# Squares of the feed-forward moved to ScalarE, the second layer's decay logits taken ahead of its query tiles, and two operand tiles cast earlier

## The chip, the cores and the metric

The kernel runs on one core of one Trainium2 chip. A core has a matrix engine (TensorE: PE in the profile, with PEld for its weight loads), three engines for elementwise work (VectorE: DVE, ScalarE: ACT, GpSimd: POOL), a queue engine that issues transfers (SyncE: SP), and DMA engines between HBM and the on-chip memories SBUF and PSUM. Each engine works through its own list of instructions in order; semaphores order the engines among each other. The metric is the time of one execution on the device in microseconds (us), lower is better.

## The reference

A sequence of 256 tokens of width 1024 goes through two stacks, in float32. The change is in the first stack alone, which has two layers of this form (the second stack, a Griffin-like and a Mamba-like layer, follows and is not touched):

```
h = layer_norm(ALPHA * h + mixed @ w_out[l], ln1_g[l], ln1_b[l])
ff = jnp.square(jax.nn.relu(h @ w_up[l])) @ w_down[l]
h = layer_norm(ALPHA * h + ff, ln2_g[l], ln2_b[l])
```

`mixed` comes from a mixer over `h @ w_in[l]`: sparse attention, gated linear attention (its decays are a log-sigmoid of small logits that are themselves a product with one tile of `h @ w_in[l]`), and a pooling branch. `w_up` is 1024x4096, `w_down` 4096x1024.

## The kernel before, in words

**Products.** Activations lie transposed, 128 features on the partitions by 256 tokens. Each float32 product is made of three half-precision ones: high weights by high operand, high weights by low operand, low weights by high operand. These are the lines L744, L745 and L746 of `split_matmul`; an output tile of 128 features over 1024 inputs takes 8 x 3 = 24 matmuls. The weights stream from HBM in slots of up to 128x2048 float32. ScalarE writes a slot's high part (`high_part`, L1768), VectorE its low part (`low_part`, L2491), TensorE may then use it (`await_slot`), and SyncE loads the slot four further on (L706). There are four slots in raw form and four in split form, so a high part is made when TensorE has finished the slot four before it. Mostly a slot is a pair of output tiles; in `down1`, whose tiles have 4096 inputs, a pair takes four slots.

**Order of the work.** The order is written out by hand: each engine has its own `first_layer(l)` for the layers l = 0 and 1, and nothing is planned at run time. A layer is the products `in1`, `out1`, `up1`, `down1`, and a layer norm behind `out1` and behind `down1` (numbered m = 0 to 3).

**Raw tiles.** The first four tiles of `up1` and of the second layer's `in1` start before the layer norm's statistics are known: they are computed from the un-normalised sum (`abreast_raw`), whose high part ScalarE makes (`raw_part`, L1808) and whose low part VectorE makes (`raw_low`, L2527). VectorE corrects these tiles in PSUM afterwards (`fix_up`, L2536 to L2548). In `down1`, ScalarE's function `behind(t)` is called after the tile pair of t; its part for t = 6 comes after the high parts of three of the four slots of the last pair. VectorE calls `raw_low` for the tiles 0 to 5 behind its residual addition of tile 5 (L2564), ahead of the low parts of the last pair's last slot and of the first slots of the next product.

**up1.** For each tile ScalarE applies relu from PSUM into `f_relu`, four tiles deep (L2040 for the four raw tiles, L1754 for the others, which wait for `f_ready`, the tile four before). VectorE squares it into the half-precision high part (L2825). GpSimd squares it once more in float32 (L3373), subtracts the high part (L3375), and raises `f_ready`; in between it scales the residual four times (L3350). Behind each pair come a high part on ScalarE and a low part on VectorE.

**Start of the second layer.** TensorE makes the raw tiles, `T_LR` (low rank of the decays, and gates), `T_GK`, `T_GQ + 1` and `T_GQ`, then `T_GV`, the decay logits (`gate_logits`, L1078), `T_GV + 1`, the transposes of the gates (`branch_gates`, L1085, which wait for the evacuation of `T_GQ`), `T_GV + 2`, `T_KC`. VectorE corrects the first two raw tiles, makes the low part of the slot held back, and corrects the other two; then it makes the low part of the slot that holds `T_KC` (`give(0)`) and adds the bias to the logits (L2669). ScalarE evacuates in the same order, makes the high part, and then the log-sigmoid: Abs L1934, Exp L1936, Ln L1939. Its evacuation of `T_GV + 1`, which frees the bank for `T_KC`, comes behind another high part.

## Time and profile before

| what | value |
|---|---|
| median of 3 runs | 1413.29 us (1413.04 to 1414.3) |
| the profiled execution's own time | 1415.02 us |
| its span, first to last instruction | 1413.2 us |
| TensorE busy | 1362.7 us, 96% |
| VectorE busy | 1056.7 us, 75% |
| ScalarE busy | 856.2 us, 61% |
| GpSimd busy | 572.3 us, 40% |
| mean granted TensorE clock | 0.993 of full |

The span is about 1.8 us shorter than the execution's own time. A busy TensorE is not one at its peak: matmuls are pipelined, each is shown with some 0.27 us although the next one starts 0.11 us later, so a stall shows as idle time that is about 0.16 us shorter than the real loss. "PEclk" is the granted clock as a share of 2.4 GHz; 0.50 is the lower of its two levels, 1.2 GHz.

### The profile page before, as it was taken

How to read it: one execution, taken by the hardware profiler on the slowest of the kernel's cores; microseconds unless marked ns; L12 is line 12 of the kernel's file. 1: busy time of each engine (PE TensorE's matmuls, PEld its weight loads, DVE VectorE, ACT ScalarE, POOL GpSimd, SP SyncE). 2: the span in 40 equal slices, each digit the busy share in tenths (PEclk: the TensorE clock that was granted, in tenths of full speed). 3: DMA queues.
4: the chain of work that ended last, by engine and by line, in shares of the span. 5: the costliest groups of instructions: out<-in, count | busy, mean ns of one | idle time of the engine just before them, and what ended most of it. 6: DMA issues, size and time to landing. Idle time of an engine off the chain costs nothing.

```text
span 1413.2 us, 31438 instructions
## 1 busy us (share of the span) xinstructions
PE 1362.7 (96%) x13296; PEld 1162.9 (82%) x13296; DVE 1056.7 (75%) x1465; ACT 856.2 (61%) x1379; POOL 572.3 (40%) x466
## 2 busy tenths in 40 slices
PE   9999999987999999999999999999999999999997
PEld 7778887876778888888777888888887778888887
DVE  6897966547797967558788798865987885898853
ACT  5685444335586544436787566554778888676552
POOL 0154996104144997115220376612222212356620
PEclk9999999999999999999999999999999999999999
DMA  9543556533443456553444265554543333466551
GB/s 360 180 150 121 179 179 226 192 131 105 165 150 121 155 204 209 197 176 106 149 150 170 107 236 196 174 190 150 174 156 124 102 120 122 178 227 217 182 181 31
DMA packets 37020, 234.64 MB, mean 166 GB/s; under 512 B 4752, under 2 KB 7824, under 8 KB 10384
## 3 DMA queue, kind: packets, MB, share of 16 engines
q1 hardware_dynamic: 36880, 232.63, 47.9%
q8 instruction: 105, 1.72, 0.5%
q14 instruction: 35, 0.29, 0.1%
HBM read 231.57 MB, written 1.05 MB: 165 GB/s over the span
## 4 chain that ended last, share of the span: by engine, by line
PE 61%; DVE 16%; POOL 10%; ACT 8%; issue 3%; DMA 1%; ACTq 0%; DVEq 0%; SPq 0%; POOLq 0%
PE psum L744 17%; PE psum L746 17%; PE psum L745 17%; DVE low L2491 5%; POOL arena L3373 4%; POOL arena L3375 4%; ACT high L1768 2%; PE psum L848 1%; PE psum L849 1%; PE psum L850 1%; POOL m L3350 1%; ACT m L2199 1%; PE psum L973 1%; DVE u L2597 1%; DMA raw<-stream 1%
## 5 line engine op out<-in xcount | busy, mean ns | idle before, releaser
L2491 DVE SCALAR_TENSOR_TENSOR low<-raw,high 128x2048 f16<-128x2048 f32 (+5 forms) x247 | 524.5, 2130 | 173.4 <-ACT high L1768 172.8
L744 PE MATMUL psum<-u,high 128*128 128x256 f16 (+2 forms) x1924 | 530.8, 276 | 15.3 <-ACT arena L1754 10.8
L745 PE MATMUL psum<-u,high 128*128 128x256 f16 (+2 forms) x1924 | 530.5, 276 | 0.0
L746 PE MATMUL psum<-u,low 128*128 128x256 f16 (+2 forms) x1924 | 530.4, 276 | 0.0
L1768 ACT ACTIVATE high<-raw 128x2048 f16<-128x2048 f32 (+4 forms) x248 | 418.1, 1690 | 118.4 <-PE psum L746 85.3
L744 PE MATMUL psum<-arena,high 128*128 128x256 f16 (+3 forms) x1208 | 332.8, 276 | 12.4 <-issue 5.3
L745 PE MATMUL psum<-arena,high 128*128 128x256 f16 (+3 forms) x1208 | 332.7, 275 | 0.0
L746 PE MATMUL psum<-arena,low 128*128 128x256 f16 (+3 forms) x1208 | 332.7, 275 | 0.0
L744 PEld LDWEIGHTS psum<-u,high 128*128 128x128 f16 x1924 | 188.4, 98 | 50.9 <-issue 13.7
L745 PEld LDWEIGHTS psum<-u,high 128*128 128x128 f16 x1924 | 188.6, 98 | 28.2 <-issue 0.7
L746 PEld LDWEIGHTS psum<-u,low 128*128 128x128 f16 x1924 | 188.5, 98 | 27.6
L3373 POOL TENSOR_TENSOR arena<-arena 128x256 f32<-128x256 f32 (+1 forms) x108 | 139.8, 1295 | 91.5 <-DVE arena L3002 87.6
L3375 POOL TENSOR_TENSOR arena<-arena 128x256 f16<-128x256 f32 (+1 forms) x108 | 160.6, 1487 | 8.5
L2986 DVE SCALAR_TENSOR_TENSOR arena<-psum,par,arena 128x271 f32<-128x271 f32 (+3 forms) x296 | 143.3, 491 | 22.4 <-ACT arena L2327 9.8
L744 PEld LDWEIGHTS psum<-arena,high 128*128 128x128 f16 (+1 forms) x1208 | 118.9, 98 | 30.7 <-issue 8.6
L745 PEld LDWEIGHTS psum<-arena,high 128*128 128x128 f16 (+1 forms) x1208 | 119.0, 99 | 17.1
L746 PEld LDWEIGHTS psum<-arena,low 128*128 128x128 f16 (+1 forms) x1208 | 119.0, 99 | 16.1
L1754 ACT ACTIVATE arena<-psum 128x256 f32<-128x256 f32 (+3 forms) x124 | 46.9, 383 | 104.1 <-POOL arena L3375 77.3
L2147 ACT ACTIVATE arena<-psum,par 128x272 f32<-128x272 f32 (+1 forms) x88 | 49.3, 570 | 80.3 <-PE psum L746 77.8
L3384 POOL TENSOR_TENSOR m<-m,rstd 128x272 f32<-128x272 f32 (+1 forms) x24 | 19.0, 791 | 138.4 <-ACT rstd L2095 138.4
L848 PE MATMUL psum<-arena,high 128*128 128x136 f16 (+2 forms) x304 | 53.3, 221 | 0.0
L850 PE MATMUL psum<-arena,low 128*128 128x136 f16 (+2 forms) x304 | 53.3, 221 | 0.0
(379 smaller groups left out, 1845.4 us busy)
## 6 DMA issues: line engine op xcount, KB each, us to landing
raw<-stream SPq DMA_DIRECT2D x206, 1024.0 KB, 4.8
raw<-stream SPq DMA_DIRECT2D x8, 768.0 KB, 4.3
raw<-stream SPq DMA_DIRECT2D x5, 512.0 KB, 4.3
raw<-stream SPq DMA_DIRECT2D x2, 896.0 KB, 4.5
con<-consts SPq DMA_DIRECT2D x1, 1437.0 KB, 12.4
h<-x_t SPq DMA_DIRECT2D x2, 512.0 KB, 5.7
raw<-stream SPq DMA_DIRECT2D x2, 448.0 KB, 5.2
misc<-small SPq DMA_DIRECT2D x1, 512.0 KB, 13.9
```

What stands on the lines that cost most here:

```text
L744: pe.matmul(out, w_hi, x[0], start=start, stop=False)
L745: pe.matmul(out, w_hi, x[1], start=False, stop=False)
L746: return pe.matmul(out, w_lo, x[0], start=False, stop=stop)
L848: pe.matmul(out, high[:, at:at + w], x[0], start=(k == 0), stop=False)
L850: return pe.matmul(out, low[:, at:at + w], x[0], start=False, stop=(k == prod["kt"] - 1))
L1754: tell(act.activation(dst, bank(BANK[g], at, at + n, rows), func, scale=scale / W_SCALE), *evac_value(g))
L1768: tell(act.activation(high[:, at:at + w], raw[:, off:off + w], ACT.Copy, scale=W_SCALE), high_ready, n=2 if half is None else 1)
L2147: tell(act.activation(buf[:, i % GATED, 0:outputs], bank(BANK[g], ahead, ahead + outputs), ACT.Identity, scale=pcol(f"ffn_w{l}", 2 * 2 * F ...
L2491: tell(dve.scalar_tensor_tensor(low[:, at:at + w], raw[:, off:off + w], W_SCALE, high[:, at:at + w], ALU.mult, ALU.subtract), split_ready ...
L2986: ins = dve.scalar_tensor_tensor(dst[:, lo:outputs], bank(BANK[g], at, at + n), weight(taps_in_all - 1 - back), dst[:, lo:outputs], ALU.mu ...
L3373: tell(pool.tensor_tensor(tmp[:, t % 2, 0:n], a[:, t % depth, 0:n], b[:, t % depth, 0:n], ALU.mult))
L3375: tell(pool.tensor_tensor(lo[:, t, 0:n], tmp[:, t % 2, 0:n], hi[:, t, 0:n], ALU.subtract), f_ready)
```

## The change

It has four parts, all in the first stack:

1. In `up1`, ScalarE squares what relu gave, in place in `f_relu`, and waits for its own relu before that. VectorE then only copies the square into half precision, and GpSimd only subtracts; its own square, its wait for itself and the buffer `f_sq` are gone. A tile's PSUM bank is free after the square instead of after relu.
2. In `down1` of the first layer (m = 1), `raw_part` for the tiles 4 and 5 comes at t = 5 instead of t = 6.
3. At the start of the second layer, VectorE adds the logits' bias ahead of `give(0)` and of the correction of the raw tiles 2 and 3. ScalarE makes `give(0)` first, evacuates `T_GV` early, does the log-sigmoid without anything in between, then evacuates `T_GV + 1` and only after it the query tiles.
4. There, TensorE transposes the gates after `T_GV + 2` instead of before it.

```
-        ff1, f_relu, f_sq = carve([(FT1, S), (4, S), (2, S)])
+        ff1, f_relu = carve([(FT1, S), (4, S)])
...
                 one(T_GV + 1)
+                one(T_GV + 2)
                 if l:
                     branch_gates()
-                one(T_GV + 2)
                 one(T_KC)
...
-                    if t == 6 and m < 2 * DEPTH - 1:
+                    if t == 6 - m % 2 and m < 2 * DEPTH - 1:
                         raw_part(m, which, l, range(4, 6))
...
                 if l:
+                    give(0)
                     act.preload_act_table_set("natural_log_exp_and_others")
                     evac(T_LR)
                     evac(T_GK)
-                evac(T_GQ + 1)
-                evac(T_GQ)
-                give(0)
+                    evac(T_GV)
+                else:
+                    evac(T_GQ + 1)
+                    evac(T_GQ)
+                    give(0)
...
                 act.wait_ge(gk_biased, l + 1)
                 tell(act.activation(gk_l, gk_x, ACT.Abs))
                 tell.settle()
                 tell(act.activation(gk_l, gk_l, ACT.Exp, scale=-1.0))
-                evac(T_GV)
+                if l == 0:
+                    evac(T_GV)
                 tell.settle()
                 tell(act.activation(gk_l, gk_l, ACT.Ln, bias=1.0), gk_logged)
+                if l:
+                    evac(T_GV + 1)
+                    evac(T_GQ + 1)
+                    evac(T_GQ)
+                    give(1)
+                    evac(T_GV + 2)
                 act.wait_ge(gates_turned, l + 1)
                 tell(act.activation(gates_t, shaped(bank(3, 0, 36), 2, 18), ACT.Exp, scale=-1.0), gates_exped)
-                give(1)
-                evac(T_GV + 1)
-                evac(T_GV + 2)
+                if l == 0:
+                    give(1)
+                    evac(T_GV + 1)
+                    evac(T_GV + 2)
...
                 def relu(t):
                     if t >= 4:
                         act.wait_ge(f_ready, FT1 * l + t - 3)
-                        evacuate(f_relu[:, t % 4, :], up + t, S, ACT.Relu)
+                        done(up + t)
+                        tell(act.activation(f_relu[:, t % 4, :], bank(BANK[up + t], 0, S), ACT.Relu, scale=1.0 / W_SCALE))
                     else:
                         act.wait_ge(fixed, 8 * l + t + 1)
-                        tell(act.activation(f_relu[:, t, :], bank(BANK[up + t], 0, S), ACT.Relu, scale=-1.0 / W_SCALE, bias=fix_w[:, t, 1:2]),
-                             *evac_value(up + t))
+                        tell(act.activation(f_relu[:, t, :], bank(BANK[up + t], 0, S), ACT.Relu, scale=-1.0 / W_SCALE, bias=fix_w[:, t, 1:2]))
+                    tell.settle()
+                    tell(act.activation(f_relu[:, t % 4, :], f_relu[:, t % 4, :], ACT.Square), *evac_value(up + t))
...
                     fix_up(f"in1_{l + 1}", (0, 1))
                     low_part(held)
-                    fix_up(f"in1_{l + 1}", (2, 3), (IN1_NTH[T_GQ + 1],))
...
-                give(0)
+                if l == 0:
+                    give(0)
                 dve.wait_ge(gk_done, l + 1)
                 for i in range(2):
                     ins = dve.tensor_scalar(shaped(gk_x, 2, S)[:, i, :], bank(7, i * S, i * S + S), pcol(f"b_gate{l}", i), None, ALU.add)
                 tell(ins, gk_biased)
                 tell.settle()
+                if l:
+                    give(0)
+                    fix_up(f"in1_{l}", (2, 3), (IN1_NTH[T_GQ + 1],))
...
-                    tell(dve.tensor_tensor(f1_hi[:, t, :], f_relu[:, t % 4, :], f_relu[:, t % 4, :], ALU.mult), fh_ready)
+                    tell(dve.tensor_copy(f1_hi[:, t, :], f_relu[:, t % 4, :]), fh_ready)
...
-                hidden_low(FT1 * l, FT1, f_relu, f_relu, 4, f1_hi, f1_lo, f_sq, S, lambda t: scaled_residual(l, t))
+                for t in range(FT1):
+                    scaled_residual(l, t)
+                    pool.wait_ge(fh_ready, FT1 * l + t + 1)
+                    tell(pool.tensor_tensor(f1_lo[:, t, :], f_relu[:, t % 4, :], f1_hi[:, t, :], ALU.subtract), f_ready)
```

Line numbers move by some 10 to 20 in the changed kernel. ScalarE's list at the end of the first layer's `down1`, before the change; `sq<-m` are squares for the layer norm, `high<-raw` the high parts, the last three of them for the next product, and L1808 the raw tiles' high parts (0 to 3, then 4 and 5):

```order
L1808 ACTIVATE arena<-m,par 128x256 x4
L1817 ACTIVATE sq<-m 128x2x256
L1768 ACTIVATE high<-raw 128x2048
L1768 ACTIVATE high<-raw 128x1792
L1768 ACTIVATE high<-raw 128x2048
L1768 ACTIVATE high<-raw 128x1024
L1808 ACTIVATE arena<-m,par 128x256 x2
```

The same place of the changed kernel:

```order
L1808 ACTIVATE arena<-m,par 128x256 x4
L1817 ACTIVATE sq<-m 128x2x256
L1808 ACTIVATE arena<-m,par 128x256 x2
L1768 ACTIVATE high<-raw 128x2048
L1768 ACTIVATE high<-raw 128x1792
L1768 ACTIVATE high<-raw 128x2048
L1768 ACTIVATE high<-raw 128x1024
```

The two rows of L1808 for the tiles 4 and 5 stand four high parts earlier. ScalarE at the start of the second layer, before the change: L1865 and L1861 to L1863 evacuate corrected raw tiles, L1754 other tiles, L1941 is the gates' exponential:

```order
L1923 ACT_TABLE_LOAD
L1865 ACTIVATE arena<-psum,lnv 96x256
L1865 ACTIVATE arena<-psum,lnv 128x256
L1861 ACTIVATE arena<-psum 64x256
L1862 ACTIVATE arena<-psum 64x256
L1863 ACTIVATE arena<-psum 128x256
L1865 ACTIVATE arena<-psum,lnv 128x256
L1768 ACTIVATE high<-raw 128x2048
L1934 ACTIVATE arena<-arena 128x512
L1936 ACTIVATE arena<-arena 128x512
L1754 ACTIVATE arena<-psum 128x256
L1939 ACTIVATE arena<-arena 128x512
```

And after it:

```order
L1768 ACTIVATE high<-raw 128x2048
L1924 ACT_TABLE_LOAD
L1865 ACTIVATE arena<-psum,lnv 96x256
L1865 ACTIVATE arena<-psum,lnv 128x256
L1754 ACTIVATE arena<-psum 128x256
L1937 ACTIVATE arena<-arena 128x512
L1939 ACTIVATE arena<-arena 128x512
L1943 ACTIVATE arena<-arena 128x512
L1754 ACTIVATE arena<-psum 128x256
L1861 ACTIVATE arena<-psum 64x256
L1862 ACTIVATE arena<-psum 64x256
L1863 ACTIVATE arena<-psum 128x256
```

The high part stands ahead of the table load, and the four evacuations of the query tiles (of which the list shows three) stand behind the log-sigmoid and the evacuation of `T_GV + 1`. ScalarE in `up1` after the change, at the raw tiles 2 and 3; before, four rows of L2040 stood directly ahead of the two high parts:

```order
L2052 ACTIVATE arena<-psum,lnv 128x256
L2054 ACTIVATE arena<-arena 128x256
L2052 ACTIVATE arena<-psum,lnv 128x256
L2054 ACTIVATE arena<-arena 128x256
L1768 ACTIVATE high<-raw 128x2048 x2
```

Each relu (L2052) is now followed by a square (L2054), so two squares of the tiles 2 and 3 have come in ahead of the high parts.

## Rows read from the trace of the kernel before

**Rows 1.** The page: shares of the chain that ended last, by engine.

```profile
PE 61%; DVE 16%; POOL 10%; ACT 8%; issue 3%; DMA 1%; ACTq 0%; DVEq 0%; SPq 0%; POOLq 0%
```

**Rows 2.** Waits from 145 to 230 us: total us, times, longest.

```profile
ACT arena L1754 <- POOL arena L3375: 38.6, 23, 4.5
```

**Rows 3.** Groups by line, 155 to 223 us: busy us, mean ns, idle before.

```profile
L2491 DVE SCALAR_TENSOR_TENSOR low<-raw,high 128x2048 f16<-128x2048 f32 x13 | 34.7, 2669 | 9.3 <-ACT high L1768 9.3
L3373 POOL TENSOR_TENSOR arena<-arena 128x256 f32<-128x256 f32 x26 | 33.6, 1293 | 0.4 <-DVE arena L2825 0.4
L3375 POOL TENSOR_TENSOR arena<-arena 128x256 f16<-128x256 f32 x26 | 28.0, 1076 | 2.0
L1768 ACT ACTIVATE high<-raw 128x2048 f16<-128x2048 f32 x13 | 24.7, 1903 | 0.0
```

**Rows 4.** TensorE alone, by stretch: us, busy, matmuls, clock, DMA.

```profile
154.94:223.34 68.40, 63.75 (x576) 1.00 0.60 203
...
308.03:314.05 6.02, 6.02 (x27) 0.50 0.85 303
474.97:543.36 68.39, 63.75 (x576) 1.00 0.61 203
543.36:546.16 2.80, 2.80 (x14) 0.50 0.77 322
```

**Rows 5.** All engines, two stretches: busy in the order PE, PEld, DVE, ACT, POOL.

```profile
250.00:300.00 50.00, 50.00 (x461) 44.81 (x459) 22.53 (x17) 21.99 (x17) 9.53 (x10) 1.00 0.46 156
...
347.34:351.60 4.26, 4.26 (x21) 2.94 (x22) 4.12 (x6) 1.80 (x4) 0.00 (x0) 0.50 0.15 23
```

**Rows 6.** Timeline, TensorE and ScalarE in and behind the first `up1`.

```profile
149.92 0.84 ACT L2040 ACTIVATE arena<-psum,lnv 128x256 f32<-128x256 f32 x2 [3.44 <-DVE psum L2545]
150.65 3.71 ACT L1768 ACTIVATE high<-raw 128x2048 f16<-128x2048 f32 x2
...
154.94 0.28 PE L744 MATMUL psum<-u,high 128*128 128x256 f16 x1 [1.22 <-DVE low L2491]
...
223.34 0.27 PE L744 MATMUL psum<-arena,high 128*128 128x256 f16 x1 [2.66 <-issue]
...
226.73 0.28 PE L744 MATMUL psum<-arena,high 128*128 128x256 f16 x1 [0.61 <-ACT arena L1754]
```

**Rows 7.** Timeline, end of the first `down1`: DVE, ACT, PE.

```profile
304.89 0.88 DVE L2527 SCALAR_TENSOR_TENSOR arena<-m,par,arena 128x256 f16<-128x256 f32 x2 [14.69 <-ACT arena L1808]
305.69 7.55 DVE L2491 SCALAR_TENSOR_TENSOR low<-raw,high 128x2048 f16<-128x2048 f32 x4
...
288.69 1.89 ACT L1768 ACTIVATE high<-raw 128x2048 f16<-128x2048 f32 x1
...
308.03 0.40 PE L744 MATMUL psum<-arena,high 128*128 128x256 f16 x1 [4.71 <-DVE low L2491]
```

**Rows 8.** Timeline, start of the second layer: ACT, PE, DVE.

```profile
329.45 1.28 ACT L1923 ACT_TABLE_LOAD   x1
...
332.15 1.12 PE L1078 MATMUL psum<-arena,misc 16*128 16x256 f32 x4
...
337.92 0.29 PE L1085 MATMUL psum<-con,arena 18*128 18x18 f32 x2 [0.96 <-ACT arena L1865]
...
347.34 0.37 PE L744 MATMUL psum<-u,high 128*128 128x256 f16 x1 [6.40 <-ACT arena L1754]
...
331.83 2.28 DVE L2491 SCALAR_TENSOR_TENSOR low<-raw,high 128x2048 f16<-128x2048 f32 x1
334.03 0.22 DVE L2536 COPY lnv<-psum 128x2 f32<-128x2 f32 x2
...
341.91 0.87 DVE L2669 TENSOR_SCALAR arena<-psum,par 128x256 f32<-128x256 f32 x2
```

**Rows 9.** Single lines: count, min/median/max ns, first and last start.

```profile
L3375 POOL TENSOR_TENSOR arena<-arena x108: 667/733/2717, 151.4 to 1352.7; 128x256 f16<-128x256 f32 x86, 128x272 f16<-128x272 f32 x22
...
L1817 ACT ACTIVATE sq<-m x16: 416/526/1058, 119.2 to 630.5; 128x256 f32<-128x256 f32 x8, 128x1024 f32<-128x1024 f32 x4, 128x512 f32<-128x512 f32 x4
```

## The prediction

> **What bounds the kernel now.** I read four views in this order. The chain that ended last comes first: 61% of it is TensorE, and 10% is GpSimd, which only does small elementwise work [rows 1]. So most of the kernel runs at TensorE's pace, and the question is where it doesn't. Then the stretches. From 250 to 300 us TensorE never stops: 461 matmuls in 50.00 us, 0.109 us each [rows 5]. In the steady part of `up1` it needs 68.40 us for 576 matmuls, in the second layer 68.39 [rows 4]; at 0.109 us these are 62.8. The third view is who waits there: ScalarE waits 38.6 us, 23 times, for GpSimd's subtraction L3375 before it may overwrite `f_relu` [rows 2]. The groups say why. GpSimd's two operations take 1.29 and 1.08 us on average, so 2.37 us a tile or 4.74 a pair. 12 pairs in 68.40 us are 5.7 us a pair; the other 1.0 is for the most part the four scalings of the residual. TensorE wants 48 x 0.109 = 5.24 [rows 3, 4]. GpSimd sets the pace of `up1`. The fourth view is the timeline at TensorE's few long stalls, those of rows 6, 7 and 8, one part of the change for each.
>
> **Part 1, the squares.** It removes GpSimd's square (L3373, 1.29 us a tile) and adds a square on ScalarE. New cost of a pair by engine, against TensorE's 5.24 us:
> - GpSimd: two subtractions. At the mean of 1.08 us that is 2.2 us, and 3.2 with the rest of 1.0. It is no longer the pace.
> - ScalarE: one high part of 1.90 [rows 3], two relus, at most 0.84 together [rows 6], and two squares. A 128x256 square takes 0.42 alone [rows 9], consecutive ones overlap by about 0.1 (two high parts of 1.90 take 3.71 [rows 3, 6]), and the wait for its own relu costs about what the overlap gives. I take 0.45 a tile, from bounds of 0.3 and 0.6. Together 3.6 us, with bounds of 3.3 and 3.9.
> - VectorE: a low part of 2.67 [rows 3] and two copies, for which the squares of before are an upper bound. No increase.
>
> So `up1` should run at 5.24 us a pair. What comes back in the first layer is 68.40 - 62.8 = 5.6 us, and the last of these stalls, 0.61 us of idle time at 226.73 or about 0.8 of real loss [rows 6]: 6.4. In the second layer it is 5.6 again, and there the stall at the start of `down1` was followed by 2.80 us at half clock [rows 4], of which 1.3 come back: 6.9.
>
> The change also costs something at one place. The stall at 154.94 is TensorE waiting for a low part, which waits for a high part at 150.65, which stands behind the relus of the raw tiles 2 and 3 [rows 6]. Two squares now stand there too: 2 x 0.45 = 0.9 us later, in both layers. Nothing hides it, since VectorE waits for the high part, here as elsewhere in this stage (9.3 us in all [rows 3]). The stall grows from 1.4 to 2.3 us. Net: 5.5 and 6.0 us.
>
> The Trainium skill speaks against this part: "ScalarE: Activation LUTs", section "Rules for kernel authors", says that relu and multiplications belong on VectorE and not on ScalarE. By that rule the square should have stayed where it was. Its sum would be 64 squares x 0.4 us = 26 us lost, if ScalarE were the pace; by the rows it has 1.3 us or more to spare in each pair.
>
> **Part 2, the raw tiles 4 and 5.** VectorE idles 14.69 us, from 290.2 to 304.89, until ScalarE's L1808 of these tiles. ScalarE has it in its list behind three high parts, the last of which waits for TensorE to free a slot. So VectorE's four low parts, 7.55 us, begin at 305.69, and TensorE stands for 4.71 us of idle time until the first of them is done at 308.03 [rows 7]. That is a real loss of 4.9 us. Behind it come 6.02 us at half clock with TensorE busy throughout [rows 4]: 3.0 us more. After the change ScalarE does the two casts at 288.7, right behind the layer norm's squares. The high part behind them is 0.8 us later, at 289.5 to 291.4, and its low part is ready at 294; TensorE wants it at 303.2. Nothing is late next: the other three high parts are paced by TensorE as before. The whole 7.9 us should come back; I take 7.8. The layer norm m = 3 has no raw tiles and m = 0 and 2 keep their order, so this is for once.
>
> **Part 3 and 4, the start of the second layer.** Times are those of the trace before, as if the 7.8 us were not gained. `T_KC` starts at 347.34 after 6.40 us of idle time (6.6 of loss), since the evacuation of `T_GV + 1` stands on ScalarE behind the log-sigmoid and a high part. The log-sigmoid stands behind the bias at 341.91 and this behind a low part and the second correction. Before it lies another stall of 0.96, for the gates' transposes [rows 8]. Afterwards:
> - ScalarE makes `give(0)` at 329.45, where the table load of 1.28 us starts now, until 331.35, and loads the table until 332.6. The logits waited for the evacuation that follows; they start at about 333.1 instead of 332.15 and take 1.12, to 334.2. `T_GV + 1` started at 334.17 behind the low part that ends at 334.11 [rows 8], and it still does. No cost.
> - VectorE: bias 334.2 to 335.1 (0.87), `give(0)` to 337.3, then the second correction. Before, that took from 334.03 to the transposes at 337.92, evacuation included: 3.9 us. So the transposes start at 341.2.
> - ScalarE: log-sigmoid 335.1 to 337.1, `T_GV + 1` evacuated at 337.5.
> - TensorE: `T_GV + 1` and `T_GV + 2` from 334.17 to 339.4, stands until 341.2, transposes, `T_KC` at 341.5 instead of 347.34.
>
> That is 5.9 us. `T_KC` also ran its first 4.26 us at half clock [rows 5], behind the long stall; 2.1 us. What is late next: `T_VC`, which TensorE reaches at 347.3, and whose low part stands behind the gates' exponential, now at 343.2 behind the query tiles and a high part of 1.9, so it is ready at about 346.3. It holds, with 1 us to spare. GpSimd still writes its eight output tiles in this stretch, and VectorE's `give(0)` may meet them: low parts that do take 2.67 instead of 2.28 [rows 3, 8]. I take 0.4 off: 7.6 us.
>
> **Sum.** 5.5 + 6.0 + 7.8 + 7.6 = 26.9 us on the profiled execution's own time, 1415.02, which leaves 1388.1. It lies 1.7 us above the median, so on the runs it is 1413.29 - 26.9 = 1386.4.
>
> One cost is uncertain by nature. Of two equal stalls, idle for 2.66 us at 223.34 and at 543.36, only the second was followed by half clock [rows 4, 6]; the stalls of 1.4 us were followed by none, those of 4.9 and 6.6 always. The two new stalls of 2.3 us lie between. I count one fall in two, at the 1.4 us that 2.80 us of half clock cost: 1387.8 us. The Trainium skill, "TensorE: Matmul & The Clock Gate", section "Part 1: The HAM clock gate", calls the monitor free-running, not tied to the kernel's start; by that rule the runs of one kernel should differ here by the odd 1 or 2 us, and the runs before, 1413.04 to 1414.3, do.
>
> **The rivals.**
> - *GpSimd stays the pace of `up1`.* A subtraction takes 0.67 us alone and up to 2.7 [rows 9], in my reading when it meets a low part. Now each pair has two of them. If both were held up, a pair would cost 5.4 us plus the rest of 1.0, 6.4, and the 11.2 us of the steady parts would not come back at all; if half of that goes, 5.6 do: 1393.4. Against it: before, four operations a pair averaged 1.19 us, so only about one in four was held up [rows 3]. The rule of the Trainium skill, "SBUF — State Buffer", section "SBUF: two separate sides", is that VectorE and GpSimd take turns at a shared port pair, whoever starts first holding it for its whole operation; it lets the copy block GpSimd too.
> - *The second layer's start gives half back.* If `give(0)` waits for one of GpSimd's operations (about 0.9 us more than my 0.4), the transposes come at 342.5, the stall there is 3.1 us and is followed by half clock again: 1.2 + 2.1 us less, 1391.1.
> - *ScalarE becomes the pace, and it is slower than before.* In `up1` ScalarE's relu, square and high part stand in one list. A pair reaches 5.24 us when the square with its wait costs (5.24 - 1.90 - 0.84) / 2 = 1.25 us. To lose all of the 26.9 us, each of the 24 steady pairs must take 1.1 us more, which is a square of 1.8 us; from there the sign turns. At 2.0 us a pair takes 6.7, 24 x 1.5 = 36 us are lost and 27 gained: 1422. For it speaks that no square behind a wait for its own engine is in the trace on this tile; against it the 0.42 us [rows 9].
> - *It does nothing.* The stalls at 308 and 347 are replaced by others behind the same slots: then only part 1 or only parts 2 to 4 would work, and for no change at all both must fail. 1413.
>
> **How the numbers follow.** Forecast 0.70, `up1` half gained 0.11, second layer half gained 0.12, ScalarE 0.03, nothing 0.04. The forecast's own spread goes from no fall of the clock and no contact with GpSimd, 1386.0, to two falls of 1.7, 1389.8; with terms that are each some tenths off, 1384 below. The range takes in the second-layer rival and part of the `up1` one: 1384 to 1392.5. A change within 0.2% (2.8 us) is about what a measurement can't tell from none. Faster 0.94, same 0.03, slower 0.03.
>
> **What the profile would show.** If I am right, in `up1` ScalarE's waits for GpSimd are gone, and 576 matmuls take 63 us behind a stall of 2.3 us (part 1); VectorE doesn't idle for over 10 us at the end of the first `down1`, and TensorE runs through at full clock (part 2); `T_KC` starts under 5 us after the end of `T_GV + 1`, with one stall of 1.8 us at the transposes (parts 3, 4). I would be wrong if a pair in `up1` took 5.5 us or more, if TensorE still stood over 3 us at the transposes, or if a stall that the trace of before hides turned up behind one of these, as at `T_VC`.

## The result, and the profile after the change

| | before | after |
|---|---|---|
| median of the runs | 1413.8 us (1413.04 to 1414.5, 4 runs) | 1390.17 us (1390.02 to 1390.2, 4 runs) |
| profiled execution, and its span | 1415.02, 1413.2 us | 1390.02, 1388.2 us |
| ratio of the times | | 0.9833, interval 0.9816 to 0.985 |

The changed kernel is 23.6 us faster on the medians, and 25.0 us on the two profiled executions. The forecast was 1387.8 us with a range of 1384.0 to 1392.5: right, and 2.4 us below the measured median.

The page of the changed kernel, busy times and the shares of the chain that ended last. Against [rows 1] GpSimd has gone from 10% to 1%, TensorE from 61% to 71%:

```profile
PE 1355.1 (98%) x13296; PEld 1161.3 (84%) x13296; DVE 1034.0 (74%) x1465; ACT 882.4 (64%) x1443; POOL 495.0 (36%) x402
...
PE 71%; DVE 15%; ACT 8%; issue 3%; POOL 1%; DMA 1%; ACTq 0%; DVEq 0%; SPq 0%; POOLq 0%
```

**The steady part of `up1`.** TensorE alone, by stretch (us, busy, matmuls, clock, DMA share, GB/s). The first and third row are the 576 matmuls of [rows 4], the second is the only stretch at half clock around the places of the change:

```profile
156.25:219.14 62.89, 62.89 (x576) 1.00 0.69 235
329.75:333.15 3.40, 3.40 (x19) 0.50 0.00 0
456.92:519.81 62.89, 62.89 (x576) 1.00 0.70 235
```

62.89 us for 576 matmuls is 0.109 us each, and busy time is equal to the length: TensorE never stands. The groups of the same stretch (busy us, mean ns, idle before it and its releaser), to be set beside [rows 3]:

```profile
L2504 DVE SCALAR_TENSOR_TENSOR low<-raw,high 128x2048 f16<-128x2048 f32 x15 | 37.3, 2489 | 14.9 <-ACT high L1768 14.9
L3441 POOL TENSOR_TENSOR arena<-arena 128x256 f16<-128x256 f32 x28 | 34.3, 1240 | 23.6 <-DVE arena L2841 23.6
...
L2054 ACT ACTIVATE arena<-arena 128x256 f32<-128x256 f32 x27 | 11.2, 416 | 0.9
L2049 ACT ACTIVATE arena<-psum 128x256 f32<-128x256 f32 x26 | 9.9, 380 | 16.8 <-PE psum L746 16.1 <-POOL arena L3441 0.7
```

L2049 is the relu and L2054 the new square. The relu's idle time is now ended by TensorE, 16.1 of 16.8 us, and GpSimd, on which ScalarE waited 38.6 us [rows 2], has 0.7 us left. GpSimd itself now idles 23.6 us.

**Ahead of tile 8.** Timeline of ScalarE (start, us, instruction). The two squares stand ahead of the high parts; the first row is the relu of tile 2, before which ScalarE idles:

```profile
150.34 0.47 ACT L2052 ACTIVATE arena<-psum,lnv 128x256 f32<-128x256 f32 x1 [2.55 <-DVE psum L2558]
...
151.17 0.46 ACT L2052 ACTIVATE arena<-psum,lnv 128x256 f32<-128x256 f32 x1
151.65 0.42 ACT L2054 ACTIVATE arena<-arena 128x256 f32<-128x256 f32 x1
151.98 3.69 ACT L1768 ACTIVATE high<-raw 128x2048 f16<-128x2048 f32 x2
```

and of TensorE:

```profile
156.25 0.28 PE L744 MATMUL psum<-u,high 128*128 128x256 f16 x1 [2.12 <-DVE low L2504]
```

The stall of [rows 6] had 1.22 us of idle time and now has 2.12.

**The end of the first `down1`.** VectorE's low parts:

```profile
286.88 2.28 DVE L2504 SCALAR_TENSOR_TENSOR low<-raw,high 128x2048 f16<-128x2048 f32 x1
289.68 2.03 DVE L2504 SCALAR_TENSOR_TENSOR low<-raw,high 128x1792 f16<-128x1792 f32 x1 [0.51 <-ACT high L1768]
```

ScalarE ahead of them:

```profile
283.71 0.89 ACT L1808 ACTIVATE arena<-m,par 128x256 f16<-128x256 f32 x2
284.51 1.90 ACT L1768 ACTIVATE high<-raw 128x2048 f16<-128x2048 f32 x1
```

The casts of the tiles 4 and 5 stand right behind the squares, VectorE's wait of 14.69 us for the casts [rows 7] is gone (0.51 us of idle time ahead of the second low part here, and at most 3.43 us later in this stage, for high parts), and TensorE's 4.71 us at this place are gone.

**The start of the second layer.** TensorE; the last two rows are the gates' transposes and the first matmul of `T_KC` (in [rows 8] at 337.92 and 347.34):

```profile
320.28 1.13 PE L1078 MATMUL psum<-arena,misc 16*128 16x256 f32 x4 [0.92 <-ACT arena L1865]
321.38 0.28 PE L744 MATMUL psum<-u,high 128*128 128x256 f16 x1
...
328.52 0.29 PE L1085 MATMUL psum<-con,arena 18*128 18x18 f32 x2 [1.73 <-ACT arena L1865]
328.75 0.28 PE L744 MATMUL psum<-u,high 128*128 128x256 f16 x1
```

ScalarE there, with the evacuation of `T_GV + 1` (L1754) ahead of those of the query tiles (L1861 to L1865):

```profile
324.22 0.38 ACT L1754 ACTIVATE arena<-psum 128x256 f32<-128x256 f32 x1
326.91 0.38 ACT L1861 ACTIVATE arena<-psum 64x256 f32<-64x256 f32 x1 [2.31 <-DVE psum L2561]
...
328.00 0.47 ACT L1865 ACTIVATE arena<-psum,lnv 128x256 f32<-128x256 f32 x1
```

The same matmul in both profiled executions tells where the time came from. The first matmul of the first layer's `T_KC` stands 0.40 us later in the one after (29.06 against 28.66; the code ahead of it is unchanged). From there:

| stretch | what the stretch gives | forecast |
|---|---|---|
| stall ahead of tile 8, first `up1` | +0.91 | +0.9 |
| the rest of that `up1`, to 226.73 before and 221.76 after | -6.28 | -6.4 |
| end of the first `down1` | -7.78 | -7.8 |
| start of the second layer, the fall of the clock at 329.75 included | -6.2 | -7.6 |
| second `up1` and what follows it, all net | -6.07 | -6.0 |

### The profile page after: what moved, and what is told of

Same layout as the page of the kernel before. It is cut to its first block, busy times and chain, and to the rows that moved or that the text cites. A ratio compares the mean times of both kernels' runs of the same rounds, so it can differ in the third digit from the quotient of the medians.

```text
span 1388.2 us, 31438 instructions
## 1 busy us (share of the span) xinstructions
PE 1355.1 (98%) x13296; PEld 1161.3 (84%) x13296; DVE 1034.0 (74%) x1465; ACT 882.4 (64%) x1443; POOL 495.0 (36%) x402
## 4 chain that ended last, share of the span: by engine, by line
PE 71%; DVE 15%; ACT 8%; issue 3%; POOL 1%; DMA 1%; ACTq 0%; DVEq 0%; SPq 0%; POOLq 0%
PE psum L744 20%; PE psum L746 20%; PE psum L745 20%; DVE low L2504 5%; ACT high L1768 2%; PE psum L848 1%; PE psum L849 1%; PE psum L850 1%; ACT m L2212 1%; PE psum L973 1%; DMA raw<-stream 1%; DVE u L2610 1%; POOL h L3402 1%; POOL m L3400 1%; DVE m L2620 1%
## 5 line engine op out<-in xcount | busy, mean ns | idle before, releaser
L2504 DVE SCALAR_TENSOR_TENSOR low<-raw,high 128x2048 f16<-128x2048 f32 (+5 forms) x247 | 518.9, 2106 | 186.6 <-ACT high L1768 186.0
L3441 POOL TENSOR_TENSOR arena<-arena 128x256 f16<-128x256 f32 x64 | 74.0, 1169 | 57.8 <-DVE arena L2841 57.8
L3391 POOL TENSOR_TENSOR arena<-arena 128x272 f16<-128x272 f32 (+1 forms) x44 | 90.5, 2058 | 3.5
L3389 POOL TENSOR_TENSOR arena<-arena 128x272 f32<-128x272 f32 (+1 forms) x44 | 58.6, 1331 | 87.6 <-DVE arena L3018 87.6
```

The costliest lines, as they stand in the source:

```text
L2504: tell(dve.scalar_tensor_tensor(low[:, at:at + w], raw[:, off:off + w], W_SCALE, high[:, at:at + w], ALU.mult, ALU.subtract), split_ready ...
L3389: tell(pool.tensor_tensor(tmp[:, t % 2, 0:n], a[:, t % depth, 0:n], b[:, t % depth, 0:n], ALU.mult))
L3391: tell(pool.tensor_tensor(lo[:, t, 0:n], tmp[:, t % 2, 0:n], hi[:, t, 0:n], ALU.subtract), f_ready)
L3441: tell(pool.tensor_tensor(f1_lo[:, t, :], f_relu[:, t % 4, :], f1_hi[:, t, :], ALU.subtract), f_ready)
```

## The experiments

Each is a short edit of the kernel before or after. Times are medians; "to after" is the median less 1390.17 us. The kernel before ran at 1414.4, 1413.87 and 1413.8 us in the three groups of runs, so such differences are good to some 0.5 us at best; a fall of the clock more or less moves a median by up to 1.7 us (below).

| run | us | ratio to before, interval | to after |
|---|---|---|---|
| part 1 alone | 1404.53 | 0.9931 (0.9916 to 0.9945) | |
| part 2 alone | 1408.15 | 0.9959 (0.9944 to 0.9974) | |
| parts 3 and 4 alone | 1406.59 | 0.9948 (0.9931 to 0.9965) | |
| part 4 undone | 1393.3 | 0.9854 (0.9839 to 0.9869) | +3.1 |
| GpSimd's squares put back | 1399.89 | 0.9901 (0.9888 to 0.9915) | +9.7 |
| two squares a tile | 1392.54 | 0.9849 (0.9835 to 0.9863) | +2.4 |
| four squares a tile | 1424.55 | 1.0075 (1.0059 to 1.0091) | +34.4 |
| square on VectorE | 1387.96 | 0.9817 (0.9803 to 0.9831) | -2.2 |
| transposes behind `T_KC` | 1390.24 | 0.983 (0.9817 to 0.9844) | +0.1 |
| first high part of `up1` early | 1383.97 | 0.9789 (0.9776 to 0.9803) | -6.2 |
| both of these | 1384.32 | 0.9791 (0.9777 to 0.9804) | -5.9 |
| both, and value tile first | 1383.43 | 0.9787 (0.9774 to 0.9799) | -6.7 |

### The parts alone

Part 1 alone, on the kernel before:

```diff
-                        evacuate(f_relu[:, t % 4, :], up + t, S, ACT.Relu)
+                        done(up + t)
+                        tell(act.activation(f_relu[:, t % 4, :], bank(BANK[up + t], 0, S), ACT.Relu, scale=1.0 / W_SCALE))
...
+                    tell.settle()
+                    tell(act.activation(f_relu[:, t % 4, :], f_relu[:, t % 4, :], ACT.Square), *evac_value(up + t))
...
-                    tell(dve.tensor_tensor(f1_hi[:, t, :], f_relu[:, t % 4, :], f_relu[:, t % 4, :], ALU.mult), fh_ready)
+                    tell(dve.tensor_copy(f1_hi[:, t, :], f_relu[:, t % 4, :]), fh_ready)
```

> Part 1 alone on the kernel before: ScalarE squares, VectorE copies, GpSimd only subtracts. If GpSimd's two operations a tile set the pace of up1 (the forecast), both up1 stages come back to TensorE's 0.109 us a matmul and the stall ahead of tile 8 grows by 0.9 us: 11.5 us less than before, so about 1402. The rival, that single subtractions held up by low parts keep GpSimd the pace, expects half of it, about 1408.

Part 2 alone:

```diff
-                    if t == 6 and m < 2 * DEPTH - 1:
+                    if t == 6 - m % 2 and m < 2 * DEPTH - 1:
```

> Part 2 alone on the kernel before: the raw tiles 4 and 5 of the first down1 are cast at t = 5. The forecast expects that TensorE's stall of 4.9 us and the 3.0 us of half clock behind it are gone: 7.8 us less, about 1406. The rival, that the stall moves to the next low part behind the same slots, expects under 3 us.

Parts 3 and 4 alone (ScalarE's half and VectorE's; TensorE's `one(T_GV + 2)` goes ahead of the gates):

```diff
+                    give(0)
...
+                    evac(T_GV + 1)
+                    evac(T_GQ + 1)
+                    evac(T_GQ)
+                    give(1)
+                    evac(T_GV + 2)
...
-                    fix_up(f"in1_{l + 1}", (2, 3), (IN1_NTH[T_GQ + 1],))
...
+                    give(0)
+                    fix_up(f"in1_{l}", (2, 3), (IN1_NTH[T_GQ + 1],))
```

> Parts 3 and 4 alone on the kernel before: the second layer's start. T_KC 5.8 us earlier after the end of the raw tiles and the half clock behind the long stall gone: 7.6 us less if the remaining stall of 2.0 us is followed by no half clock, 6.2 if it is, as in the changed kernel. A sum of the three kernels of this call that falls well short of the whole change (23.6 us) would mean that the parts share a cause.

They give 9.9, 6.3 and 7.8 us against 1414.4 us. The sum, 24.0, is the whole change's 23.6 within the noise: the parts add up. Parts 1 and 2 lie 1.6 and 1.5 us under what was expected of them, while the matmuls of their profiles moved as expected (part 1 by 5.5 us in the first layer and 6.0 in the second, part 2 by 7.8). About the price of one fall of the clock (below) is missing in each; that it is the cause is not shown. Part 1 alone leaves the stall at the end of `down1` as it was:

```profile
302.60 0.40 PE L744 MATMUL psum<-arena,high 128*128 128x256 f16 x1 [4.72 <-DVE low L2493]
```

Part 2 alone has ten microseconds there without a gap and at full clock:

```profile
302.00:312.00 10.00, 10.00 (x87) 1.00 0.61 210
```

In parts 3 and 4 alone, TensorE's wait at the transposes is the one of the whole change:

```profile
340.39 0.29 PE L1085 MATMUL psum<-con,arena 18*128 18x18 f32 x2 [1.72 <-ACT arena L1865]
```

Yet the stretch behind it is at full clock, where the whole change had half clock (and the stall at 308.54, still there without part 2, is followed by 3.1 us at half clock where the kernel before had 6.0, so this profile gains 1.4 us that are no part of the change):

```profile
340.40:344.00 3.60, 3.60 (x33) 1.00 0.10 36
```

### Part 4 undone

TensorE does the gates between `T_GV + 1` and `T_GV + 2` again; the rest is the changed kernel.

```diff
                 one(T_GV + 1)
-                one(T_GV + 2)
                 if l:
                     branch_gates()
+                one(T_GV + 2)
```

> The changed kernel with part 4 alone undone: the gates' transposes stand ahead of T_GV + 2 again. They must wait for the query tiles' evacuation at 328.5, so TensorE stands from 324.0 on, 4.5 us instead of 2.0, and does T_GV + 2 afterwards: 2.6 us more than the changed kernel, and with a longer half clock 3 to 4 us more, 1393 to 1394. The rival, that the order on TensorE is of no account since ScalarE's list sets T_KC, expects no difference.

It costs 3.1 us: the tile of 2.6 us no longer covers the wait for the log-sigmoid and the corrections. The wait at the transposes grows from 1.73 to 4.34 us:

```profile
330.13 0.29 PE L1085 MATMUL psum<-con,arena 18*128 18x18 f32 x2 [4.34 <-ACT arena L1865]
```

So part 4 is a part of the gain by itself.

### GpSimd's squares put back

The squares stay on ScalarE, and GpSimd does its old one too, whose result nobody uses. That tells whether the gain came from GpSimd's shorter list, or from VectorE's lighter copy or the later release of the bank.

```diff
+                    tell(pool.tensor_tensor(f_sq[:, t % 2, :], f_relu[:, t % 4, :], f_relu[:, t % 4, :], ALU.mult))
+                    tell.settle()
                     tell(pool.tensor_tensor(f1_lo[:, t, :], f_relu[:, t % 4, :], f1_hi[:, t, :], ALU.subtract), f_ready)
```

> The changed kernel, and GpSimd squares each tile once more into a spare buffer and waits for it, as before the change; the result isn't used. ScalarE and VectorE do what they do in the changed kernel. If GpSimd's time a tile was what up1 waited for, all of the gain of up1's steady parts goes: 11 us or more over the changed kernel, 1401 to 1404, with ScalarE waiting for GpSimd again. The rival, that VectorE's lighter copy or the later release of the bank made the gain, expects under 3 us.

1399.89 us: 9.7 us are gone again (11 and more was expected). Its waits from 145 to 230 us (total us, times, longest) have ScalarE's for GpSimd back, if not all of the 38.6 us [rows 2]:

```profile
ACT arena L2049 <- POOL arena L3443: 22.3, 12, 2.7
```

And TensorE needs 67.2 and 67.5 us for the steady parts of the two layers instead of 62.9:

```profile
155.89:223.12 67.23, 64.85 (x577) 0.98 0.61 206
460.86:528.38 67.52, 63.97 (x577) 1.00 0.61 205
```

The first of them has a fall of the clock in it, 3.4 us at half clock behind the stall at tile 8 (hence 0.98), so waiting for GpSimd cost 2.6 us there and 4.6 in the second layer, against 5.5 in both before the change. A second fall, from 224.10 us, stands behind the 2.24 us of idle time at the start of `down1`; the changed kernel had one fall in all, so 1.7 of the 9.7 us are the price of one fall more. GpSimd's time is most of what part 1 won, and ScalarE's only had to be free. GpSimd's two operations cost as much as before here (0.88 and 1.52 us on average in that stretch, 2.40 a tile against 2.37), but the scalings of the residual take 6.1 us instead of 8.0. That this is the rest of the difference is likely and not shown.

### More squares on ScalarE

One more square with its wait in each tile, into a spare buffer, ahead of the real one:

```diff
+                    for i in range(1 if True else 0):
+                        tell(act.activation(f_sq[:, i % 2, :], f_relu[:, t % 4, :], ACT.Square))
+                        tell.settle()
```

> The changed kernel, and ScalarE squares every tile of up1 once more into a spare buffer, with a wait behind it; the result isn't used. If a square with its wait costs 0.45 us and the steady pairs have 1.3 us or more to spare, 0.9 us more a pair is hidden there, and only the chain ahead of tile 8 pays: 0.9 us more in each layer, 1392, some tenths to 3 us more if half clock follows. If ScalarE is already the pace, 24 pairs cost 0.9 us more each: 1412.

1392.54 us, 2.4 more. The steady part of the first layer does not change (62.9 us from 156.75 us on), and at tile 8 TensorE waits 3.01 us instead of 2.12, which is 0.45 us for each of the two squares, in both layers:

```profile
156.75 0.28 PE L744 MATMUL psum<-u,high 128*128 128x256 f16 x1 [3.01 <-DVE low L2507]
```

Then three more a tile, from the fifth tile on, so that the place ahead of tile 8 is left alone (`range(3 if t >= 4 else 0)`):

> The changed kernel with three more such squares on ScalarE for each tile of up1 from the fifth on, results unused. 2 x 3 x 0.45 = 2.7 us more a pair on ScalarE: 3.6 + 2.7 = 6.3 us against 5.24, so ScalarE becomes the pace and about 1 us is lost on each of some 26 pairs: 1410 to 1418. If it stays within 3 us of the changed kernel, the square is much cheaper than 0.45 us or the spare time larger than I said.

1424.55 us: here is the rival that ends slower than before, and at a higher price than expected. ScalarE's list of a pair (L2055 are the three extra squares):

```profile
204.86 0.36 ACT L2049 ACTIVATE arena<-psum 128x256 f32<-128x256 f32 x1
205.26 1.31 ACT L2055 ACTIVATE arena<-arena 128x256 f32<-128x256 f32 x3
206.60 0.42 ACT L2057 ACTIVATE arena<-arena 128x256 f32<-128x256 f32 x1
206.92 1.89 ACT L1768 ACTIVATE high<-raw 128x2048 f16<-128x2048 f32 x1
...
210.79 0.36 ACT L2049 ACTIVATE arena<-psum 128x256 f32<-128x256 f32 x1
```

It has no gap, and from 204.86 to 210.79 it is 5.93 us for a pair instead of 5.24; a square with its wait is (206.60 - 205.26) / 3 = 0.45 us. TensorE waits once in each pair:

```profile
211.02 0.27 PE L744 MATMUL psum<-u,high 128*128 128x256 f16 x1 [0.52 <-ACT arena L2057]
```

And then it waits at a place that I had not counted, the start of `down1` ("issue" is a wait for which the profile shows no releaser):

```profile
234.68 0.37 PE L744 MATMUL psum<-arena,high 128*128 128x256 f16 x1 [6.41 <-issue]
```

In the first layer that is 11 pairs x 0.7 = 8 us, 6.4 us at the start of `down1`, and half clock around it. In the second layer nine waits at pairs, one of them of 2.13 us, lose about as much (7.5 us), and the start of `down1` waits 6.40 us again; together 29 of the 34 us. Falls of the clock behind tile 8 (157.38) and behind the 2.13 us (481.65) cost 1.7 each besides. A ScalarE that is the pace leaves its backlog to the stage behind, which the expectation left out.

### The square on VectorE

The other engine for the square, at the same precision: VectorE squares in place and then casts, ScalarE has its relu alone.

```diff
-                        tell(act.activation(f_relu[:, t % 4, :], bank(BANK[up + t], 0, S), ACT.Relu, scale=1.0 / W_SCALE))
+                        tell(act.activation(f_relu[:, t % 4, :], bank(BANK[up + t], 0, S), ACT.Relu, scale=1.0 / W_SCALE), *evac_value(up + t))
...
-                    tell.settle()
-                    tell(act.activation(f_relu[:, t % 4, :], f_relu[:, t % 4, :], ACT.Square), *evac_value(up + t))
...
+                    tell(dve.tensor_tensor(f_relu[:, t % 4, :], f_relu[:, t % 4, :], f_relu[:, t % 4, :], ALU.mult))
+                    tell.settle()
                     tell(dve.tensor_copy(f1_hi[:, t, :], f_relu[:, t % 4, :]), fh_ready)
```

> The changed kernel with the square on VectorE instead of ScalarE: VectorE squares f_relu in place in float32, waits for itself and copies into half precision; GpSimd subtracts as in the changed kernel. By the rule that multiplications belong on VectorE: the high part ahead of tile 8 is 0.9 us earlier in each layer, 1388.4 or, with the half clock gone too, 1387. By my rows: VectorE's pair becomes a low part of 2.67, two squares of 0.41 to 0.83 and two copies of 0.3 to 0.8, 4.1 to 5.9 us, so at or over TensorE's 5.24; I expect 1388 to 1394.

1387.96 us, 2.2 us below the changed kernel. Groups from 155 to 218 us:

```profile
L3441 POOL TENSOR_TENSOR arena<-arena 128x256 f16<-128x256 f32 x28 | 47.8, 1714 | 11.5 <-DVE arena L2841 11.5
L2502 DVE SCALAR_TENSOR_TENSOR low<-raw,high 128x2048 f16<-128x2048 f32 x15 | 36.1, 2405 | 0.7 <-ACT high L1768 0.7
...
L2839 DVE TENSOR_TENSOR arena<-arena 128x256 f32<-128x256 f32 x29 | 18.7, 644 | 0.0
```

VectorE's square takes 0.64 us where ScalarE's takes 0.42, GpSimd's subtraction goes from 1.24 to 1.71 us, VectorE has 0.7 us of idle time left ahead of its low parts instead of 14.9, and TensorE still needs only 62.89 us for the steady part. What it wins is the place where the squares don't stand: at tile 8 TensorE waits 1.22 us again, in both layers, which is 1.8 of the 2.2 us.

```profile
155.06 0.28 PE L744 MATMUL psum<-u,high 128*128 128x256 f16 x1 [1.22 <-DVE low L2502]
```

The square that is 0.22 us faster on ScalarE stood in the list that was late. The Trainium skill, "ScalarE: Activation LUTs", section "Rules for kernel authors", which puts multiplications on VectorE, gives the better kernel here, though not for a shorter operation: VectorE's square is the longer one, and the steady part has room for either. The prediction took that rule to mean that the square should stay where it was; the float32 square was on GpSimd, and what the rule asks for is this kernel.

### Shorter stalls

Two edits aim at the two stalls that the change left. The first moves the transposes behind `T_KC`, in the second layer:

```diff
                 one(T_GV + 2)
+                if l == 0:
+                    one(T_KC)
                 if l:
+                    one(T_KC)
                     branch_gates()
-                one(T_KC)
```

> The changed kernel, but TensorE transposes the second layer's gates behind T_KC instead of ahead of it. T_KC's low part and bank are ready some 2 us before the transposes' input is, so the stall of 2.0 us and the half clock behind it (1.4 us) should go: 3.0 to 3.4 us less, about 1387. ScalarE's exponential of the gates stands behind a high part anyway and isn't delayed. The rival: T_KC waits for its low part instead, and nothing or under 1 us is gained.

1390.24 us, no gain, where 3.0 to 3.4 us were expected: a miss. The wait is gone from the trace, for the transposes follow with no idle time:

```profile
333.17 0.29 PE L1085 MATMUL psum<-con,arena 18*128 18x18 f32 x2
```

but the profiled execution (1390.93 us) has half clock twice, behind the 2.1 us at tile 8 and again from 324.0, behind waits of only 0.93 us at 322.14 and 0.26 us at 323.54. In both places the changed kernel had full clock:

```profile
156.80:160.20 3.40, 3.40 (x19) 0.50 0.85 272
324.00:327.40 3.40, 3.40 (x19) 0.51 0.88 299
```

The runs of this kernel lie between 1387.49 and 1391.02 us, while those of the changed kernel lie within 0.2 us: the fastest is 2.7 us below it. So the count of falls differs from run to run. Each run's mean granted clock bears it out: 0.998 at 1387.49 us, 0.997 at 1389.55, 0.996 at 1390.93 and 1391.02, and one fall of 3.4 us to half clock is 0.0012 of the mean.

The second edit gives ScalarE the first high part of `up1` between the raw tiles 1 and 2:

```diff
-                    if n == 1 and not name.startswith("out1"):
+                    if n == 0 and name.startswith("up1"):
+                        high_part(i + SPLIT)
+                    if n == 1 and not name.startswith(("out1", "up1")):
                         high_part(i - 1 + SPLIT)
```

> The changed kernel, but in up1 ScalarE makes the high part of tiles 8 and 9 between the raw tiles 1 and 2, where it idles 3.4 us, instead of behind the squares of 2 and 3. If the stall of 2.4 us ahead of tile 8 is only that chain (squares, high part, low part), it goes to 0.3 us or less in both layers: 4.2 to 4.6 us less than the changed kernel, 1385.8. If VectorE's list (the second correction and the copies, ahead of the low part) is late too, under 2 us come back.

1383.97 us, 6.2 us below the changed kernel; 4.2 to 4.6 were expected. ScalarE idled 2.55 us ahead of the relu of tile 2; the high part now fills this time:

```profile
147.56 1.90 ACT L1768 ACTIVATE high<-raw 128x2048 f16<-128x2048 f32 x1
150.19 0.47 ACT L2054 ACTIVATE arena<-psum,lnv 128x256 f32<-128x256 f32 x1 [0.74 <-DVE psum L2560]
```

The stall at tile 8 is gone in both layers, and no matmul of the profiled execution is at half clock (the last 5 us of the span, in which TensorE has nothing to do, are, as at the end of every run here):

```profile
0.00:1376.90 1376.90, 1353.07 (x13296) 1.00 0.50 170
```

Two stalls of 2.3 us and one fall of 1.7 make 6.3; the expectation had left out the fall. The wait at the transposes is still there, 1.45 us, with full clock behind it.

Both edits together:

> Both of the former edits on the changed kernel: about 1390.2 - 4.4 - 3.2 = 1382.6 us if they are additive, which they should be since they lie in different products.

1384.32 us, no better than the one, where 1382.6 was expected. The stall at the transposes has moved behind them, to the transposed values' matmuls L1093, which wait for the evacuation of `T_GV + 2`:

```profile
328.84 0.87 PE L1093 MATMUL psum<-con,arena 128*128 128x128 f32 x6 [0.96 <-ACT arena L1756]
```

That evacuation (at 328.41) stands on ScalarE behind the high part of `give(1)`:

```profile
326.61 1.91 ACT L1770 ACTIVATE high<-raw 128x2048 f16<-128x2048 f32 x1
328.41 0.38 ACT L1756 ACTIVATE arena<-psum 128x256 f32<-128x256 f32 x1
```

So these two change places:

```diff
-                    give(1)
                     evac(T_GV + 2)
+                    give(1)
```

> The kernel with the early high part in up1 and the gates' transposes behind T_KC, and in addition ScalarE evacuates T_GV + 2 ahead of the high part give(1). The stall of 1.2 us that took the place of the one at the transposes waits for just this evacuation, so it should go: 1.0 us less than with both edits (1384.3), 1383.3. If the next low part (T_VC's) is late by then, nothing is gained.

1383.43 us (1383.04 to 1384.75, 5 runs). The 0.96 us are gone and a smaller wait for the next low part, `T_VC`'s, has come in, 0.40 us at 331.45.

This is the fastest median of all, 30.4 us below the kernel before. The three last kernels can't be told from each other by these runs; they beat both kernels of the study, and what they have in common is the early high part.

## Why the prediction was right, and where its 2.4 us went

**The pace of `up1` (part 1).** Right in what comes back. 576 matmuls take 62.89 us where 62.8 was forecast, in both layers, and ScalarE waits 0.7 us for GpSimd. That it was in the main GpSimd's time is shown by putting its squares back: its waits come back, at 2.6 and 4.6 of 5.5 us a layer. The picture of a GpSimd that takes 5.7 us for every pair was too even. The four scalings, which make up the rest beside the 4.74 us, were these (one line more of the view of [rows 3]):

```profile
L3350 POOL TENSOR_SCALAR m<-h 128x512 f32<-128x512 f32 x4 | 8.0, 1999 | 0.0
```

That is 0.7 us a pair, so 5.4 and not 5.7. Of TensorE's 4.6 us of idle time in the 68.40 us, 2.66 are the one stall at 223.34, at whose end the 68.40 us stop: GpSimd's backlog showed for the larger part at the start of `down1`, the same place that the expectation of four squares left out. The cost at tile 8 was forecast at 0.9 and measured at 0.91; doubling the squares added another 0.9.

**The two lists.** A pair on ScalarE was forecast at 3.6 us, with 0.45 for a square and its wait. By the means of the groups it is 1.90 + 2 x 0.38 + 2 x 0.42 = 3.5 us, and the square with its wait is 0.45 in the tight list of four squares. GpSimd's pair, forecast at 3.2 us, is 2 x 1.24 and the residual's 0.5 (6.2 us for its four scalings): 3.0.

**Part 2.** Right: 7.8 forecast, 7.78 measured between the same matmuls, 6.3 on the medians when alone.

**Parts 3 and 4.** `T_KC` was forecast 5.9 us earlier, beyond what part 2 gives. It starts at 328.75 instead of 347.34, 18.6 us earlier, of which 12.8 were there already at the first matmul behind the logits (334.17 to 321.38): 5.8. The stall at the transposes was forecast at 1.8 us and has 1.73. Moving the table load and the logits cost nothing, as forecast: the logits wait 0.92 us, and `T_GV + 1` behind them does not start later for it. The 0.4 us taken off for a contact with GpSimd did not come (the low part of `give(0)`, at 322.36 us, took 2.35 us against 2.28). The term was 7.6 and 6.2 came, because the clock fell behind this stall, at 1.7 us; without it 7.9 would have come.

**The fall of the clock.** The prediction counted one fall in two, at 1.4 us, behind the new stalls at tile 8. The number is right and the place is not: there was one, 3.40 us at half clock or 1.7 lost, behind the stall at the transposes, for which I had counted none. That one was counted and one came is luck. Behind a stall of 2.1 us at tile 8 the clock fell in 4 of 12 cases over all the kernels, one in three and not one in two (last section).

**What failed** is the last step of the sum, "so on the runs it is 1413.29 - 26.9". The terms were made on the profiled execution, 1415.02 us. On its basis they give 1415.02 - 26.9 + 1.4 = 1389.5, and 1390.02 was measured: 0.5 us off. But one of them, the 1.3 us of half clock at 543.36 (2.80 us, so 1.4 rather), is a thing of that execution: an equal stall in the first layer had none [rows 4, 6]. The runs of the parts show it outright. This stall is unchanged in part 2 alone and in parts 3 and 4 alone; it was followed by 0.50 of the clock in the first (from 536.62 us) and by 1.00 in the second (from 534.57 us). So 1.7 us were first taken off as what the profiled execution lies above the median, and then this half clock was counted as a gain against the median too. The 2.4 us are these 1.7, 0.5 from the terms (0.40 of start, 0.3 for a fall that costs 1.7 and not 1.4, and 0.1 in the first `up1`, less 0.3 that the second layer's start gave beyond its term), and 0.15 between the execution after and its median. That the unprofiled runs of the kernel before had one fall less is inferred; the mean granted clocks of the later runs of this kernel fit it, 0.994 or 0.995 in all fourteen below 1414 us and 0.993 in six of the ten above.

**The rivals.**
- *GpSimd stays the pace* fell: its subtraction did become slower, 1.24 us on average instead of 1.08, but two of them leave it 23.6 us idle. With the square on VectorE it is 1.71 us and TensorE still doesn't stand. The rule of the Trainium skill, "SBUF — State Buffer", section "SBUF: two separate sides", that the two engines take turns, agrees: GpSimd's operation is slowest on average where VectorE has only 0.7 us of idle time left, and single operations show it (last section). It decides nothing here.
- *The second layer gives half back* was half true: no contact with GpSimd made the stall longer (1.73 us), but half clock followed it. 1391.1 us was its time, and it lies 0.9 us from the measured one, nearer than my 2.4; the sum of it, though, has a stall of 3.1 us that isn't there.
- *ScalarE becomes the pace and it is slower* exists, with four squares a tile. I had put the turn at 1.8 us for the square work of a tile. Four squares are 4 x 0.45 = 1.8, and the kernel is there already 10.8 us slower than before, though a pair took 5.93 us and not the 6.3 of the sum: the turn comes earlier, since the backlog also falls on `down1`.
- *It does nothing* fell: each part alone has its own gain.

## What to carry to other kernels

Read who ends the wait of the engine that feeds the bottleneck, take work off that one, and then look at what the new home's list has standing behind the work: here the faster engine for the square was the worse one, because one high part behind it was late, and moving this high part into an idle gap of 2.55 us gave more (6.2 us) than the choice of engine (2.2). A stall of TensorE is worth closing whole, since one of 2 us may be followed by half clock and cost nearly double. If terms are read from one profiled execution, price what is particular to it (half clock behind a stall that an equal stall lacks) against that execution, and not against the median of the runs.

## What the runs showed of the hardware that was not expected

- The granted clock does not follow from the length of a stall alone. Behind 2.1 us of idle time at tile 8 it was half in 4 of 12 cases. Behind 1.7 us at the transposes it was half in the changed kernel and with two squares a tile, and full with parts 3 and 4 alone, with GpSimd's squares and with the square on VectorE. Once, with the transposes behind `T_KC`, it fell behind waits of 0.93 and 0.26 us. Behind 4.3 us and more it was half each time, 9 of 9. The Trainium skill, "TensorE: Matmul & The Clock Gate", section "Part 1: The HAM clock gate", calls the monitor free-running; equal stalls with unequal ends agree with that.
- Each stretch at half clock behind a stall of up to 3.0 us was 3.4 us long. Where TensorE was busy throughout, as at 329.75 in the changed kernel, one costs 1.7 us; where part of it fell into the stall itself it cost less (2.80 us of matmuls at half clock at 543.36 before the change, 1.4 us). In the kernel with two squares a tile there were two, from 329.5 and from 459.2 us, the second behind the 3.01 us at tile 8 of the second layer; the same 3.01 us in the first layer had none.
- VectorE's low part and GpSimd's subtraction did not run side by side: whichever started second took longer, by about the time for which the other still ran. Both orders, in the kernel with the square on VectorE (in the second pair of rows the two subtractions are merged; the first takes 0.70 us and the second begins at 179.09 and takes 2.71):

```profile
156.60 2.28 DVE L2502 SCALAR_TENSOR_TENSOR low<-raw,high 128x2048 f16<-128x2048 f32 x1
156.76 2.65 POOL L3441 TENSOR_TENSOR arena<-arena 128x256 f16<-128x256 f32 x1 [0.23 <-DVE arena L2841]
...
178.43 3.38 POOL L3441 TENSOR_TENSOR arena<-arena 128x256 f16<-128x256 f32 x2
178.53 2.75 DVE L2502 SCALAR_TENSOR_TENSOR low<-raw,high 128x2048 f16<-128x2048 f32 x1
```

  A subtraction that meets nothing takes 0.67 us and a low part 2.28. So the averages of 1.08, 1.24 and 1.71 us are mixtures of operations of about 0.7 and about 2.7 us.
- The first matmul of the first layer's `T_KC` came between 28.61 and 29.61 us in the 14 profiled executions, behind the same code. So up to 1 us between two of them can be nothing but the start.
